# Where layer 0's expert mix keeps its dense outputs: six PSUM banks to the end, and SBUF accumulators for the fetched rows

## The reference

```python
def block(hb):
    ...
    sc, pos = lax.top_k(cand, PEER_TOPK)
    eidx = jnp.take_along_axis(cidx, pos, axis=-1)
    gw = jax.nn.softmax(sc, axis=-1)
    a = jnp.einsum('thkd,td->thk', u_tab[eidx], hb)
    w = (jax.nn.gelu(a.astype(jnp.float32), approximate=False) * gw).astype(hb.dtype)
    return jnp.einsum('thk,thkd->td', w, v_tab[eidx])
...
x = x + mod[5] * _peer(h, ...)
```

## Time and profile before

| | |
|---|---|
| median of 3 runs | 5169.08 us (5167.35 to 5171.95) |
| profiled execution | 5142.85 us, its span 5141.0 us |
| granted TensorE clock, mean | 0.897 |
| PE busy | 4198.6 us (82%) |
| DVE busy | 3266.5 us (64%) |
| POOL busy | 1419.4 us (28%) |
| ACT busy | 1323.8 us (26%) |
| bytes moved by DMA | 1254.78 MB, mean 244 GB/s |

### The profile page before, as it was taken

The page is one execution under the profiler, slowest core; times in us unless marked ns, Lnnn a source line. Parts: engine busy times, 40 slices in busy tenths (PEclk is TensorE's granted clock), DMA queues, the critical chain, the costliest instruction groups (busy, mean ns, idle before and its releaser), DMA issues. The chain is left out here.

```text
span 5141.0 us, 59219 instructions
## 1 busy us (share of the span) xinstructions
PE 4198.6 (82%) x21780; PEld 3188.4 (62%) x21780; DVE 3266.5 (64%) x6621; ACT 1323.8 (26%) x2531; POOL 1419.4 (28%) x1387
## 2 busy tenths in 40 slices
PE   6977688779999998587888777756789998777786
PEld 5864687676666666344544463534678887666675
DVE  3145774319997778577887823493349967555565
ACT  2125222213444655000000021421223565400000
POOL 0000331003332445344444300060004334344341
PEclk8989898889999999698999887957889999988997
DMA  4120101237987999999999710133249999899995
GB/s 165 58 76 31 40 5 33 90 116 290 320 330 266 402 404 414 361 391 384 390 392 389 294 32 19 18 103 82 66 153 375 336 347 414 335 405 402 403 403 232
DMA packets 469170, 1254.78 MB, mean 244 GB/s; under 512 B 52094, under 2 KB 191092, under 8 KB 463252
## 3 DMA queue, kind: packets, MB, share of 16 engines
q0 software_dynamic: 184320, 671.17, 33.9%
q1 hardware_dynamic: 277944, 570.82, 30.4%
q10 hardware_dynamic: 6620, 9.01, 0.5%
HBM read 1147.59 MB, written 103.25 MB: 243 GB/s over the span
## 5 line engine op out<-in xcount | busy, mean ns | idle before, releaser
L1942 PE MATMUL banks<-acts_in,v_rows 128*128 128x384 f32 (+1 forms) x4096 | 1164.1, 447 | 300.7 <-DMA v_rows<-peer_v 173.2
L1942 PEld LDWEIGHTS banks<-acts_in,v_rows 128*128 128x128 f32 x4096 | 799.4, 197 | 665.1 <-DMA v_rows<-peer_v 193.9
L1565 PE MATMUL banks<-h_dense,u_t 128*128 128x384 f32 (+1 forms) x4096 | 1200.0, 437 | 0.0
L1539 POOL DMA_INDIRECT rows<-peer_u,expert x640 | 633.1, 989 | 1619.2 <-DVE weight L1842 805.8
L1565 PEld LDWEIGHTS banks<-h_dense,u_t 128*128 128x128 f32 x4096 | 748.3, 193 | 246.0 <-issue 2.4
L1842 DVE CUSTOM_DVE_ANT_0 rows<-rows,banks 128x1024 f32<-128x1024 f32 x640 | 765.4, 1211 | 194.1 <-DMA rows<-peer_u,expert 129.6
L1924 POOL DMA_INDIRECT v_fetched<-peer_v,expert x640 | 606.8, 948 | 861.1 <-DVE banks L2004 746.7
L2004 DVE SCALAR_TENSOR_TENSOR banks<-v_fetched,weight,banks 128x1024 f32<-128x1024 f32 x630 | 784.1, 1281 | 0.0
L1980 DVE TENSOR_TENSOR acts_in<-acts_in,gates 128x384 f32<-128x384 f32 (+1 forms) x256 | 124.8, 488 | 430.8 <-DMA acts_in<-activations 430.6
L1933 ACT COPY y_tok<-banks 128x1024 f32<-128x1024 f32 x5 | 5.1, 1012 | 1461.4 <-DVE banks L2004 1461.4
L1624 ACT COPY u_t<-banks 128x512 f32<-128x512 f32 x512 | 299.9, 586 | 289.2 <-PE banks L1556 286.4
(11 more groups left out here) (444 smaller groups left out, 5688.6 us busy)
## 6 DMA issues: line engine op xcount, KB each, us to landing
u_raw<-peer_u SPq DMA_DIRECT2D x256, 512.0 KB, 7.9
v_rows<-peer_v SPq DMA_DIRECT2D x256, 512.0 KB, 15.2
gate_table<-part SPq DMA_DIRECT2D x20, 2048.0 KB, 11.7
activations<-acts SPq DMA_DIRECT2D x128, 192.0 KB, 5.8
gates<-gate_table SPq DMA_DIRECT2D x8, 3072.0 KB, 22.8
acts_in<-activations SPq DMA_DIRECT2D x128, 192.0 KB, 12.2
peer_wq_in<-peer_wq SPq DMA_DIRECT2D x16, 1024.0 KB, 5.3
ada_ring<-ada_w SPq DMA_DIRECT2D x32, 512.0 KB, 4.1
```

Of the source, the lines that this page charges most:

```text
L1539: pool.indirect_dma_start(out=ring[:, s % U_RING, :], out_offset=None, in_=rows_of_u, in_offset=bass.IndirectOffsetOnAxis(ap=expert[:, t, ...
L1565: last = nc.tensor.matmul(out, u_t[:, i % 2, k * P:(k + 1) * P], h[:, k], start=(k == 0), stop=(k == DK - 1))
L1942: return nc.tensor.matmul(y_at(m if RESIDENT else j // GROUP * DK + m), v[:, j % V_ROWS, m * P:(m + 1) * P], acts[:, j % V_ROWS], start=st ...
```

## The change

In both layers the dense outputs now stay in PSUM until the end. Layer 0's 8 x 384 columns lie one behind another in six banks (`y_at`), so that some blocks cross a bank's edge; `pieces` cuts such a block into two matmuls of 128 and 256 columns. TensorE goes row by row in both layers, and x_t is added in eight additions after the last group. The accumulators of the fetched rows (`acc`) move for layer 0 from PSUM to a new SBUF tile, row_sums; layer 1 keeps its own in PSUM (WHOLE). Before the last transposes TensorE now waits for the additions in both layers.

```diff
-    RESIDENT = ND * DK <= BANKS * BANK
+    assert ND * DK <= 6 * BANK
+    WHOLE = ND * DK <= BANKS * BANK
...
+        sums = None if WHOLE else a.sb("row_sums", [P, 2, D])
...
         def acc(half):
-            return ps[:, ACC + half * D:ACC + (half + 1) * D]
-
-        def y_at(u):
-            at = u % DK * ND if RESIDENT else u % BANKS * BANK
-            return ps[:, at:at + ND]
+            return ps[:, ACC + half * D:ACC + (half + 1) * D] if WHOLE else sums[:, half]
+
+        def y_at(m):
+            return ps[:, m * ND:(m + 1) * ND]
+
+        def pieces(m):
+
+            edges = [m * ND] + [b for b in range(0, 8 * BANK, BANK) if m * ND < b < (m + 1) * ND] + [(m + 1) * ND]
+            return list(zip(edges, edges[1:]))
...
-                    sp.wait_ge(y_done, groups_done(i - V_ROWS // GROUP + 1))
+                    sp.wait_ge(y_done, i - V_ROWS // GROUP + 1)
...
-                else:
                     for m in range(DK):
-                        u = i * DK + m
-                        if u >= BANKS:
-                            pe.wait_ge(y_added, u - BANKS + 1)
-                        for r in range(GROUP):
-                            if m == 0:
-                                ready(i * GROUP + r)
-                            last = product(i * GROUP + r, m, r == 0, r == GROUP - 1)
-                        last.then_inc(y_done, 1)
+                        for lo, hi in pieces(m):
+                            last = nc.tensor.matmul(ps[:, lo:hi], v[:, j % V_ROWS, m * P:(m + 1) * P],
+                                                    acts[:, j % V_ROWS, lo - m * ND:hi - m * ND],
+                                                    start=(j == 0 and lo % BANK == 0),
+                                                    stop=(j == KEYS - 1 and hi % BANK == 0))
+                last.then_inc(y_done, 1)
             pe.wait_ge(summed, NG)
-            if not RESIDENT:
-                pe.wait_ge(y_added, GROUPS * DK)
+            pe.wait_ge(y_added, DK)
...
-                    if u and not RESIDENT:
-                        add(u - 1)
-            if RESIDENT:
-                for m in range(DK):
-                    add(m)
-            else:
-                add(GROUPS * DK - 1)
+            for m in range(DK):
+                add(m)
```

More of the change, by code:

```diff
@@ L1889, in acc @@
         def acc(half):
-            return ps[:, ACC + half * D:ACC + (half + 1) * D]
-        def y_at(u):
-            at = u % DK * ND if RESIDENT else u % BANKS * BANK
-            return ps[:, at:at + ND]
+            return ps[:, ACC + half * D:ACC + (half + 1) * D] if WHOLE else sums[:, half]
[4 more added lines that the diff above has]
+            return list(zip(edges, edges[1:]))
         def turned_at(t):
             return ACC + t * D if t < 2 else (t - 2) * D
-        def groups_done(count):
-            return count if RESIDENT else count * DK
         @block.sync
@@ L1939, in ready @@
                 pe.wait_ge(weighted, j + 1)
-            def product(j, m, start, stop):
-                return nc.tensor.matmul(y_at(m if RESIDENT else j // GROUP * DK + m),
-                                        v[:, j % V_ROWS, m * P:(m + 1) * P], acts[:, j % V_ROWS], start=start, stop=stop)
             for i in range(GROUPS):
-                if RESIDENT:
-                    for j in range(i * GROUP, (i + 1) * GROUP):
-                        ready(j)
-                        for m in range(DK):
-                            last = product(j, m, j == 0 and m * ND % BANK == 0,
-                                           j == KEYS - 1 and (m + 1) * ND % BANK == 0)
-                    last.then_inc(y_done, 1)
-                else:
-                    for m in range(DK):
-                        u = i * DK + m
-                        if u >= BANKS:
-                            pe.wait_ge(y_added, u - BANKS + 1)
-                        for r in range(GROUP):
-                            if m == 0:
-                                ready(i * GROUP + r)
-                            last = product(i * GROUP + r, m, r == 0, r == GROUP - 1)
-                        last.then_inc(y_done, 1)
+                for j in range(i * GROUP, (i + 1) * GROUP):
+                    ready(j)
+                    for m in range(DK):
+                        for lo, hi in pieces(m):
[4 more added lines that the diff above has]
+                last.then_inc(y_done, 1)
             pe.wait_ge(summed, NG)
-            if not RESIDENT:
-                pe.wait_ge(y_added, GROUPS * DK)
+            pe.wait_ge(y_added, DK)
             for t in range(NG):
@@ L1980, in multiply, with add @@
                 nc.vector.tensor_tensor(x, x, gates[:, b % 2, :, r, :], ALU.mult).then_inc(weighted, 1)
-            def add(u):
-                dve.wait_ge(y_done, GROUPS if RESIDENT else u + 1)
-                if u == 0:
+            def add(m):
+                dve.wait_ge(y_done, GROUPS)
+                if m == 0:
                     dve.wait_ge(x_loaded, 16)
-                m = u % DK
                 x = g.x_t[:, m, col:col + ND]
-                nc.vector.scalar_tensor_tensor(out=x, in0=y_at(u), scalar=g.mod[:, layer, 40 + m, stream:stream + 1],
+                nc.vector.scalar_tensor_tensor(out=x, in0=y_at(m), scalar=g.mod[:, layer, 40 + m, stream:stream + 1],
                                                in1=x, op0=ALU.mult, op1=ALU.add).then_inc(y_added, 1)
```

## The result

The changed kernel takes 5126.93 us (median of four runs, 5117.05 to 5129.47), the kernel before 5170.07 (four runs, 5167.35 to 5171.95): a ratio of 0.9913, 95% interval 0.9896 to 0.9931, 43 us less. The forecast was 28 us less, 5141 us, and its range began at 5128, 1 us above the measured median. The direction and the place were right, the size was not. A later comparison (e9) gave 5125.21 against 5164.3, ratio 0.9916 (0.9903 to 0.9929).

A forecast was written before the change was run, and what follows sets the result against it. The prediction took transferred bytes, with holes in the DMA queues, to bound layer 0's mix. Terms: -34 for transfers, +3 held fetches, +3 the end, -28 in all: 5169 - 28 = 5141 us, range 5128 to 5168.

The forecast's parts named there:

- The ceiling is bytes: Layer 0's mix: transfers, not an engine, set the limit; at layer 1's 402 GB/s they take 801.6 us, not 837.5.
- the ramp: First slices of layer 0's mix, at 174 and 358 GB/s: 2 us of slow start that stays.
- small holes: After gate loads in layer 0's mix: held GpSimd fetches leave small gaps in the transfers, +3 us.
- The end: +3: End of layer 0's mix: 14 row sums and 8 additions, 20.9 us against 17.5 from last landing, +3 us.
- the hold: Layer 0's indirect DMAs wait for VectorE's row sums with two SBUF inputs; median above 1.2 us, +3 us.
- TensorE's stops of 3 to 5 us per gate load: Layer 0's mix: TensorE stops 3 to 5 us per gate load instead of 17, near 99 us between loads.
- Short matmuls: Blocks cut at a bank's edge in layer 0: 0.329 us a pair, 0 to 10 us more, hidden under DMA.
- rival C: Shared port slows layer 0's fetches, deciding from 2.18 us mean spacing: slower, 5205 to 5236 us; chance 0.10.
- Wrong if VectorE waits over 20 us for fetched rows: Sign against the forecast: VectorE's waits for fetched rows, 0.0 before, exceeding some 20 us in all.
- B: Holes after gate loads stay; only the start's 10 us go, less 3: -7, 5162 us; chance 0.20 with half-way cases.
- A: The forecast: layer 0's DMA filled as in layer 1, 5141 us, own range 5130 to 5153; chance 0.70.

The follow-up runs named there:

- e9: The changed kernel, unchanged, run once more: median 5125.21 us, ratio 0.9916 to the kernel before.
- e7: The kernel before with only layer 0's row sums moved to SBUF: mix 865.5 us, ratio 1.0005 to the kernel before.
- e5: The changed kernel with TensorE's old order in layer 0, column block outside and four rows inside: mix 825.5 us, ratio 0.9941 to the kernel before.
- e6: The kernel before with layer 0's x_kept loaded behind the first expert row instead of the eighth: mix 847.7 us, ratio 0.9986.
- e3: The changed kernel with one PSUM accumulator for layer 0's fetched rows instead of two in SBUF: mix 812.6 us, ratio 0.9908 to the kernel before.
- e1: The changed kernel with 248 idle additions put back on VectorE, no other engine waiting for them: mix 812.2 us, ratio 0.9912 to the kernel before.

## Why the prediction was right in its mechanism and wrong in its size

Taking the table in order, the 46 us of the mix come about so: the sums in SBUF alone, +11 (e7); the outputs in six banks and the additions gone, with the old order of TensorE, -40 (e5 against e7); row by row, -17 (the changed kernel against e5). The -40 holds several things together: the wait of TensorE, the additions' VectorE time, and the wait for x_kept, for which e6 has 7 us.

- **"The ceiling is bytes": held.** The prediction had 801.6 us for the bytes at layer 1's rate, plus 2 for the ramp and 3 for small holes. From the first fetch to the last landing it took 802.4 us (2911.7 - 2109.3), against 839.4 before: -37, where -31 was forecast. Of these 6 us 2 are a misreading: the last packet before ended at 2925.5, not at 2923.5. The rest is the allowance of 2 us for the ramp and 3 us for the held fetches, most of which did not show. This is 6 of the 18 us of error in the mix.
- **"The end: +3": the step that failed.** The prediction put 20.9 us of row sums and additions behind the last landing. It started this chain at the wrong event. The chain took 21.4 us, as worked out, but it starts at the last multiplication, and from there it took 23.05 before. From the last landing to the end it was 15.5 us before and is 6.1 now: -9 in place of +3, the other 12 us. I had read the landing and line 2025, not the last multiplication ahead of both, and took the distance between them, 17.5 us with the landing misread, for the chain. (In the sum the misreading cancels: it made the end of the kernel before 2 us too long and its transfers 2 us too short.)
- **Why the last multiplication moved further ahead of the landing** (15.4 us instead of 7.6): by e3 it is not the hold, since without it the distance is 14.6 us; by e1 it is not VectorE's free time, since with VectorE busy for 81% of the mix instead of 67% the distance is 14.0; by e5 it is the order of TensorE, since with m outside it is 7.0. It is 6.0 to 8.5 us in all the kernels with m outside. The DMA queues show what goes with it. Row by row the dense loads are over early: their last packet of 1 KB or more starts 29 us before the last landing in the changed kernel, 28 in e3 and 29 in e1, and fetches alone are left; with m outside it starts 7 us before it in the kernel before, 5 in e5. Why the order of TensorE lets the dense loads run so far ahead is not shown; I take it that y_done comes earlier, and no run varied the share of the two queues by itself. The fetches left over cost nothing, since they land one by one ahead of their row sums, the last of them by 0.7 us.
- **TensorE's stops of 3 to 5 us per gate load: wrong, harmless.** They are 9.7 to 11.9 us. The row behind the gates lands late and TensorE has used up what was loaded. From gate load to gate load it is 96.7 to 98.6 us after the first cycle (96.8 from 2297.18 to 2393.94), where 99 was forecast.
- **Short matmuls: held.** 60.61 us for 279 records at 2139.73 are 0.217 us a record, 5.2 us for a row of 24, as for the 16 records of before at 0.328.
- **GpSimd: the hold exists, its form was misjudged.** Around 2886 us of the changed kernel:

```profile
2884.58 3.67 DVE L1993 SCALAR_TENSOR_TENSOR row_sums<-v_fetched,weight,row_sums 128x1024 f32<-128x1024 f32 x3
...
2886.13 1.74 POOL L1927 DMA_INDIRECT v_fetched<-peer_v,expert  x1 [0.66 <-DVE row_sums L1993]
2888.17 0.55 DVE L1970 TENSOR_TENSOR acts_in<-acts_in,gates 128x384 f32<-128x384 f32 x1
2888.17 1.36 POOL L1927 DMA_INDIRECT v_fetched<-peer_v,expert  x1 [0.30 <-issue]
...
2889.84 0.94 POOL L1927 DMA_INDIRECT v_fetched<-peer_v,expert  x1 [0.30 <-issue]
```

  Some fetches are held (1.74, 1.36), others go through in 0.94. Which of them is decided by when a fetch starts: in the changed kernel's mix every fetch that started between 0.11 and 1.1 us into a row sum lasted until 0.81 us after that row sum's end, and all 46 that started in its first 0.07 us took 0.94 us while it ran. The prediction had each fetch start some 0.37 us into a row sum. The median is 0.942 us (1.007 in e9), where over 1.2 was forecast; the mean is 1.228. The mean spacing is (2895.2 - 2109.3)/383 = 2.05 us, under the 2.18 from which rival C would have decided. The Trainium skill, "SBUF — State Buffer", section "Who interferes with whom", has the later instruction of such a pair wait until the first one ends. The held fetches agree: that of 1.74 us ended 0.81 us after the row sum under which it started. The 46 that ran through beside a row sum would have to be the first of their pair by that rule; the row sums beside them lasted 1.28 us on average, like the others.
- **"Wrong if VectorE waits over 20 us for fetched rows": a bad sign to look for.** It waited 104.8 us in 145 waits, and the kernel was faster than forecast. With a full DMA some engine must wait for it, and which one does says nothing about the speed.
- **The rivals.** B (holes behind gates stay, -7) is excluded for the change, but its first half is what e6 measured: 7 us for the hole at the start alone. C is excluded by the spacing; e7 shows that its mechanism is real, with 11 us, in the form where VectorE has no gap behind a gate load. Of A, the forecast, the mechanism is the one measured; its own range, 5130 to 5153, misses the median by 3 us.

## What to carry to other kernels

When a stage is bound by transfers, read what holds up the order to issue the next load, not the busy engine: 153 us of extra VectorE work cost 4 us in the changed kernel, while taking the same work out of the old form, and with it TensorE's wait for it and the wait for x_kept, gained 40. A consumer that can start with the first of four loaded rows is worth as much care as the number of buffers: counted from the kernel with its sums in SBUF, eight banks in rotation gained 20 us, six resident ones 40, and the order of the loops 17 more. And find the last event on which the chain at a stage's end really hangs, before adding work to the chain: measured from the landing it looked 12 us worse than it was.

## What the runs showed of the hardware that was not expected

- The first weighted row of a token tile (TENSOR_SCALAR, 1024 float32) takes 0.748 us with its output in SBUF (changed kernel) and 1.287 with it in PSUM (e3). The three-operand form took 1.28 either way. The Trainium skill, "VectorE: DVE Perf Modes", section "Mode 2×_2P — use both read ports for one tensor", says that a single-source operation with all operands in SBUF runs twice as fast even in float32; this ratio of 1.7 agrees.

```profile
L1993 DVE SCALAR_TENSOR_TENSOR row_sums<-v_fetched,weight,row_sums x378: 1270/1280/1325, 2149.8 to 2912.4; 128x1024 f32<-128x1024 f32 x189
L1991 DVE TENSOR_SCALAR row_sums<-v_fetched,weight x6: 747/748/754, 2144.8 to 2668.7; 128x1024 f32<-128x1024 f32 x6
```

- Indirect DMAs issued against a stream of two-SBUF-input operations had means of 1.23 us (changed), 1.36 (e7) and 1.39 (e1), against 0.96 with PSUM sums (e3). Whether one is held is decided by its start, as told above: 0.11 us or more into a row sum it is, up to 0.07 us it is not.
- Row sums in one PSUM accumulator are 1.39 us apart (e3), in two SBUF ones by turns 1.20.
- Fetches alone, with no dense loads beside them, moved as much as both together: 409 GB/s at a share of 1.03 (102.7%) from 2895 to 2903 in the changed kernel, where one queue has all the packets, and 410 from 2919 to 2923 in the kernel before. The fall to 240 and 224 GB/s that follows is the tail of the last few.

```profile
DMA packets 900, 3.27 MB, mean 409 GB/s; under 512 B 101, under 2 KB 101, under 8 KB 900
q0 software_dynamic: 900, 3.27, 102.7%
```
